# Base inverse step of a chunked delta-rule kernel as four fused multiply-adds, one a token tile, in place of one product and one sum over all four tiles

## The reference

```python
def _gated_delta_rule(q, k, v, g, beta):
    ...
    a_mat = jnp.where(strict, jnp.einsum('bhncd,bhnsd->bhncs', k_beta, k) * decay, 0.0)
    eye = jnp.eye(CHUNK, dtype=a_mat.dtype)
    t_mat = lax.linalg.triangular_solve(eye + a_mat, jnp.broadcast_to(eye, a_mat.shape),
                                        left_side=True, lower=True)
    u = jnp.einsum('bhncs,bhnse->bhnce', t_mat, v * beta[..., None])
    w = jnp.einsum('bhncs,bhnsd->bhncd', t_mat, k_beta * jnp.exp(g)[..., None])
    ...
    def step(s, inp):
        q_c, k_c, u_c, w_c, qk_c, gt = inp
        v_new = u_c - jnp.einsum('bhcd,bhde->bhce', w_c, s)
        o = jnp.einsum('bhcd,bhde->bhce', q_c, s) + jnp.einsum('bhcs,bhse->bhce', qk_c, v_new)
        s = s * gt[..., None, None] + jnp.einsum('bhcd,bhce->bhde', k_c, v_new)
        return s, o
```

## Time and profile before

| | |
|---|---|
| median of 3 runs | 1106.7 us (1106.35 to 1107.34) |
| the profiled execution | 1106.26 us, its span 1104.1 us |
| TensorE busy | 1068.6 us, 97% of the span |
| VectorE busy | 688.1 us, 62% |
| ScalarE busy | 532.2 us, 48% |
| mean granted TensorE clock | 0.995 |

### The profile page before, as it was taken

How to read it: one execution, slowest core, us unless ns; L and a number is a source line. 1 busy time by engine, 2 the same in 40 slices (tenths; PEclk the granted TensorE clock), 3 DMA queues, 4 the chain that set the end, 5 groups by cost and what they waited for, 6 DMA issues and landing times. The chain is left out here.

```text
span 1104.1 us, 19488 instructions
## 1 busy us (share of the span) xinstructions
PE 1068.6 (97%) x7212; PEld 848.8 (77%) x7212; DVE 688.1 (62%) x2078; ACT 532.2 (48%) x1557; POOL 121.7 (11%) x160
## 2 busy tenths in 40 slices
PE   7999999989999999999999999999999999999997
PEld 5877777767878787777877878787786878787775
DVE  5285959575655747576365765748456575758554
ACT  4556665644736444363354536344454546463300
POOL 3513122123200000020000000002000000002320
PEclk9999999999999999999999999999999999999999
DMA  8957475655652726253562551724544353612332
GB/s 278 315 202 258 167 264 193 240 181 182 227 195 87 243 83 228 89 183 98 175 203 110 194 180 58 249 74 157 156 151 153 126 160 119 229 62 75 115 104 87
DMA packets 58285, 183.54 MB, mean 166 GB/s; under 512 B 8464, under 2 KB 21200, under 8 KB 44880
## 3 DMA queue, kind: packets, MB, share of 16 engines
q1 hardware_dynamic: 51392, 173.13, 45.4%
q10 hardware_dynamic: 6800, 9.18, 2.9%
HBM read 138.22 MB, written 44.07 MB: 165 GB/s over the span
## 5 line engine op out<-in xcount | busy, mean ns | idle before, releaser
L827 PE MATMUL bank<-xr,w 128*128 128x512 f32 x2496 | 656.4, 406 | 7.8 <-DVE xr L1527 7.8
L827 PEld LDWEIGHTS bank<-xr,w 128*128 128x128 f32 x2496 | 450.5, 189 | 103.1 <-issue 10.6
L878 PE MATMUL bank<-wo,y_split 128*128 128x512 f32 x432 | 114.4, 404 | 0.0
L878 PEld LDWEIGHTS bank<-wo,y_split 128*128 128x128 f32 x432 | 77.0, 189 | 14.6 <-issue 0.7
L1575 DVE SCALAR_TENSOR_TENSOR kq<-conv_in,convw_all,kq 128x512 f32<-128x512 f32 x96 | 76.1, 794 | 8.6 <-ACT conv_in L1169 6.4
L1478 ACT ACTIVATE o_scaled<-bank 128x128 f32<-128x128 f32 x64 | 17.7, 276 | 125.6 <-PE bank L1099 125.3
L1331 ACT ACTIVATE score<-score,neg_max 128x256 f32<-128x256 f32 (+1 forms) x128 | 62.7, 493 | 17.6 <-DVE neg_max L1747 17.6
L1781 DVE TENSOR_TENSOR y_step<-blocks,y_cols 128x60 f32<-128x60 f32 (+14 forms) x240 | 49.9, 208 | 20.0 <-DMA blocks<-n_spill 11.7
L1909 DVE TENSOR_SCALAR steps<-bank,nb_rk 128x128 f32<-128x128 f32 x64 | 22.3, 348 | 64.2 <-PE bank L1095 64.2
L1912 DVE SCALAR_TENSOR_TENSOR state<-state,cols_all,bank 128x128 f32<-128x128 f32 x64 | 22.2, 347 | 62.7 <-PE bank L1098 62.7
L761 POOL TENSOR_TENSOR xr<-y_tile,xr 128x256 fp32r<-128x256 f32 x8 | 6.0, 772 | 457.0 <-ACT xr L1150 457.0
(11 more groups left out here) (217 smaller groups left out, 1637.3 us busy)
## 6 DMA issues: line engine op xcount, KB each, us to landing
w<-w_split SPq DMA_DIRECT2D x78, 1024.0 KB, 5.6
w_split<-w SPq DMA_DIRECT2D x26, 1024.0 KB, 4.9
blocks<-n_spill ACTq DMA_DIRECT2D x32, 256.0 KB
y_spill<-y_out SPq DMA_DIRECT2D x30, 256.0 KB, 5.4
x_tile<-w_in SPq DMA_DIRECT2D x13, 512.0 KB, 5.8
y_tile<-w_in SPq DMA_DIRECT2D x12, 512.0 KB, 5.9
y_tile<-y_spill SPq DMA_DIRECT2D x12, 512.0 KB, 6.2
x_tile<-x SPq DMA_DIRECT2D x12, 512.0 KB, 3.9
```

The lines of the kernel that those rows point to most:

```text
L827: ins = nc.tensor.matmul(bank[JOBS[at].bank][:], w[:, turn % 3, wp, k, :], xr[:, xp, k], start=(step == 0), stop=(step == 3 * KT - 1))
L878: ins = nc.tensor.matmul(bank[JOBS[at].bank][:], y_place(t)[:, yp, k], wo[:, k, wp, half * UNIT:(half + 1) * UNIT], start=(step == 0), sto ...
```

## The change

A step j of the base inverse is four SCALAR_TENSOR_TENSOR instructions, one for each tile c, each of which multiplies by `y_cols[:, c, j]` (one value per partition) and adds in one pass. `y_step` is no longer used here. The even tiles wait on `base_step`: tile 0 for tiles 0 and 1 of the step before, tile 2 for tiles 2 and 3 of it. The odd tiles and all tiles of step 0 do not wait on it.

```diff
-        base_step = counter("base_step", 2 * (BASE - 1))
+        base_step = counter("base_step", CH * (BASE - 1))
...
                     rest = slice(j + 1, BASE)
-                    wide = [P, CH, BASE - 1 - j]
-                    if j > 0:
-                        after(dve, base_step, n, 2 * j)
-                    nc.vector.tensor_tensor(y_step[:, :, rest], blocks[:, j, :, j + 1:],
-                                            y_cols[:, :, j:j + 1].to_broadcast(wide), ALU.mult).then_inc(base_step.sem, 1)
-                    after(dve, base_step, n, 2 * j + 1)
-                    start = ident16[:, rest].unsqueeze(1).to_broadcast(wide) if j == 0 else y_cols[:, :, rest]
-                    nc.vector.tensor_tensor(y_cols[:, :, rest], y_step[:, :, rest], start, ALU.add).then_inc(base_step.sem, 1)
-                after(dve, base_step, n, 2 * (BASE - 1))
+                    for c in range(CH):
+                        if j > 0 and c % 2 == 0:
+                            after(dve, base_step, n, CH * (j - 1) + c + 2)
+                        start = ident16[:, rest] if j == 0 else y_cols[:, c, rest]
+                        nc.vector.scalar_tensor_tensor(y_cols[:, c, rest], blocks[:, j, c, rest], y_cols[:, c, j:j + 1], start,
+                                                       ALU.mult, ALU.add).then_inc(base_step.sem, 1)
+                after(dve, base_step, n, CH * (BASE - 1))
```

## The result

The changed kernel takes 1125.3 us (median of 4 runs, 1124.1 to 1129.7) against 1107.0 for the kernel before, measured beside it (4 runs, 1106.4 to 1107.5). The ratio is 1.0179, 95% interval 1.0158 to 1.0200; the quotient of the two medians, 1.0165, lies inside it. The forecast was 1123, with a range of 1109 to 1130. The profiled execution took 1125.6 us, with a span of 1123.5, 19.4 more than before.

The account below looks back on a forecast made before the run. TensorE was taken as the bound, so VectorE's change counts only where TensorE waits at L1045 for the transpose. 1.61 us a slot, less free delay and stalls, sums to 16.6; 1106.26 + 16.6 = 1122.9, predicted 1123, range 1109 to 1130.

Parts of the forecast that it names:

- Free-running instructions and their price: VectorE's base_inverses: no even tile waits, so 60 instructions cost their free-running spacing, 8.47 us a slot against 6.87.
- the fixed part: Share of a VectorE instruction's spacing that is there whatever its length: 0.131 us with a per-partition scalar, bounds 0.066 and 0.131.
- Rival 4: VectorE's base_inverses: every second instruction held until its predecessor has written, 11.7 us a slot, 1167 us; chance 0.04.
- rival 1: VectorE's base_inverses: the per-partition scalar costs nothing in the stream, 4.6 us instead of 6.87, 1098 us; chance 0.10.
- All of the delay counts: TensorE at L1045: delay beyond each slot's free share is added in full, neither caught up nor counted twice; 16.6 us.
- the 16.6 us: Sum over the 16 slots of the delay of TensorE's weight load L1045 behind the transpose.
- Rival 3: Half of the delay is absorbed as TensorE's later waits in the slot shrink: about +8, 1115 us; chance 0.10.
- the late slots: Slots 12, 13, 14: TensorE waits and a stall hides the first half's loss, so 3 x 0.95 = 2.9 us.
- TensorE's own busy time stays: Sign in the profile: TensorE's busy time, 1068.6 us before, does not change.
- GpSimd's share: Slots 0 to 2: GpSimd's subtraction may slow one more short instruction, about 0.5 us each, 1.6 in all, outside the sum.
- the stall at j = 8: Function's wait for the second half of blocks; in slots 4, 12, 13, 14 it hides the first half's 0.66 us.
- The small signs: VectorE's busy time rises by 25 to 35 us; L1045's wait rises to about 30 us in 14 or 15 slots.

Follow-up runs that it names:

- Experiment 1: Changed kernel with the per-partition scalar replaced by a constant, count, length and order of instructions kept: 1095.8 us, ratio 0.9903.
- experiments 2 and 3: Kernel before with eight, then four, short products behind the last step, a delay of 1.6 or 0.8 us a slot: 1130.7 and 1117.5 us.
- before, convs behind (7): Kernel before with the convolutions convs(n, 0.2) moved behind base_inverses: 1108.2 us, ratio 1.0004.
- two chains, convs behind (8): Kernel before with wide instructions cut into two alternating chains and the convolutions moved behind base_inverses: 1105.6 us, ratio 0.9988.
- two chains, early convs (9): Kernel before with two alternating chains and the convolutions moved behind base_inverses in slots 0 to 2 alone: 1102.7 us, ratio 0.9947.
- two chains (5): Kernel before with each wide instruction cut into two pairs of tiles in alternating chains, 60 plain instructions a slot: 1101.8 us, ratio 0.9956.
- later place (4): Changed kernel with the places of the lowest level in the slot moved back, more dense matmuls ahead of L1045: 1126.5 us, ratio 1.0180.
- after, convs behind (6): Changed kernel with the convolutions convs(n, 0.2) moved behind base_inverses: 1124.0 us, ratio 1.0139.
- after, GpSimd done (10): Changed kernel in which slots 0 to 2 wait for the last of GpSimd's subtractions before the function begins: 1132.0 us, ratio 1.0214.

## Why the prediction was right, point by point

**Free-running instructions and their price.** Held. No even tile waited, the fixed part was 0.130 for a forecast of 0.131, the function 8.38 us for 8.47. Rival 4 (every second one held, 11.7 us a slot) is out. Experiment 1 shows the other branch: with a constant the fixed part is 0.070 and the time 1095.8, near rival 1's 1098. The Trainium skill, Vector Engine (DVE) Microarchitecture Reference, section Measured stream behaviour on trn2, gives about 75 ns per instruction; this case agrees for instructions without a per-partition scalar (0.070) and not for those with one (0.130).

**All of the delay counts.** Right in direction and as the cause, as experiments 2 and 3 show: the pure delay reproduces the loss, and half the delay loses about half. But the 16.6 us were said to be idle time of TensorE, and that grew by 11.1 only; the other 8.3 are the clock. Rival 3's time (half absorbed, 1115) is out; its mechanism, smaller waits later in the slot, shows as no more than 1.7 us (L1045's wait grew by 12.8, TensorE's idle time by 11.1). How much later L1045 comes in each slot than before, beyond the slot before (from its weight loads; 1.58 for slot 0 is 79.88 - 78.30):

```
slots                   forecast   measured
0, 1, 2, 3, 7, 11       9.7        1.58 + 2.79 + 3.43 + 2.70 + 1.76 + 1.83 = 14.1
12, 13, 14              2.9        0.12 - 1.82 - 0.91 = -2.6
4                       0.6        2.7
5, 6, 9, 10             2.4        0.53 + 0.49 + 0.52 + 0.68 = 2.2
8                       0.0        1.3
15                      1.0        0.9
to L1045 of slot 15     16.6       18.6 (0.8 more from there to the end)
```

About 6 of the 14.1 us in the first line are busy time of TensorE, as are the 1.3 of slot 8, so the waiting in the six slots of the first line came to about 8 for the forecast 9.7. Two terms were missed, with opposite signs: the clock (+8.3) and the late slots (-2.6 for +2.9). That the total came within 3 us is in part luck.

**Missed: the clock.** "TensorE's own busy time stays" failed: 1076.9 for 1068.6, +8.3 us, nearly half of the loss. Over all the profiles the same 7212 matmuls take the longer, the lower the granted clock, and on the whole, though not in each pair, the clock is lower where L1045 waits longer (us of wait for the transpose, granted clock, TensorE's busy us):

```
constant (1)                 3.2    0.998   1066.3
before, convs behind (7)     7.1    0.997   1067.6
two chains, convs behind (8) 8.2    0.996   1067.8
two chains, early convs (9) 10.5    0.994   1069.7
two chains (5)              12.1    0.995   1069.1
before                      13.4    0.995   1068.6
later place (4)             18.3    0.991   1073.2
delay of 0.8 (3)            20.0    0.993   1073.0
after, convs behind (6)     20.2    0.987   1076.6
after                       26.2    0.987   1076.9
delay of 1.6 (2)            29.0    0.982   1082.2
after, GpSimd done (10)     32.6    0.985   1077.5
```

In the kernels before and after every stretch at a low clock inside the slots stands right behind a wait for the transpose, two before and six after. The trace that the prediction was made from had the sign of it: the wait of 3.00 us in slot 3 has a granted clock of 0.66 over the 5 us behind it. Of the increments above, those of slots 1 to 3 hold the most of it: slot 1 came 2.79 us later where 1.6 had been said, 1.5 of that as busy time, slot 2 3.43 later with 2.8 of it. Of L1045's waits the shortest with a lower clock right behind it was 1.87 us, but longer ones left the clock at 1.00: 2.33 us ahead of slot 11 and 2.89 ahead of slot 4, 2.94 and 2.92 in experiment 10 and, before the change, 2.19 ahead of slot 13. In slot 2 of experiments 4 and 6 the clock fell to 0.50 for some us behind another wait, 1.05 us for the attention weights (L950), after several waits close together. So the length of the wait alone does not decide it; what else does is not settled here.

**GpSimd's share: as named in slots 0 to 2, and overlooked in slot 3.** Beside GpSimd the first four instructions take 1.6 us more than in slot 5 in slot 0 and 1.0 more in slots 1 and 2, and experiment 10 shows the cause. But the old function had lost 1.0 us to it in each of these slots as well. From its first start to the spreading product it went from 7.85 to 9.98 us in slot 0, from 7.85 to 9.43 in slot 1 and from 7.84 to 9.42 in slot 2. That is 2.1, 1.6 and 1.6 more, where the prediction had 1.61 and up to 0.5 on top. Slot 3, which the prediction did not name here, stands under GpSimd too: the function takes 10.54 us there before and 12.72 after, 2.2 more, beside two groups of four instructions of GpSimd. During the second group 7 of the new instructions run, in the equally long stretch behind it 23, with the DMA engines busy in both (first GpSimd's second group; then two stretches, their us, the busy us and count of these VectorE instructions, the clock, the DMA share and GB/s):

```profile
242.36 2.86 POOL L761 TENSOR_TENSOR wo<-x_tile,wo 128x256 fp32r<-128x256 f32 x4 [0.99 <-ACT wo L1164]
...
242.36:245.22 2.86, 2.86 (x7) 1.00 1.01 337
245.22:248.08 2.86, 2.86 (x23) 1.00 0.83 328
```

This is the slot with the longest wait of L1045, 3.00 us before and 5.14 after.

**Missed: the late slots.** In slots 12 to 14 the forecast let the stall at j = 8 stand and fall by 0.66 us. It was nearly gone (0.29 us at step 8 of slot 12, none in slot 13), and the three slots gave back 2.6 us instead of costing 2.9. The stall moved about in every run: the idle time of the function for `blocks` is 11.7 us before, 4.8 after, 7.4 with the delay of 1.6 and 14.0 with the constant. The prediction had also left out that the start waited for the first half of `blocks` in slots 4, 12, 13 and 14, 0.9 to 1.3 us each, 4.4 of the 11.7 us before; behind such a wait VectorE being late costs nothing either. In slot 4 it went the other way: the start waited 3.13 us (0.94 before), step 8 only 0.27:

```profile
314.09 0.67 DVE L1782 SCALAR_TENSOR_TENSOR y_cols<-blocks,y_cols,ident 128x15 f32<-128x15 f32 x4 [3.13 <-DMA blocks<-n_spill]
```

A landing taken from one execution is no fixed point for another. Why the blocks land when they do in these slots was not tested, and it leaves some us of experiment 10 and of the late slots unexplained.

**The small signs.** VectorE's busy time rose by 42 us, not 25 to 35: the waiting pairs had left more small gaps than I had counted. In slot 5 the function went from 5.77 to 8.35 us busy, and 16 times that difference is 41. L1045's wait came to 26.2 us in 15 slots where about 30 in 14 or 15 had been said.

## What to carry to other kernels

Fusing a product and a sum pays by what an instruction costs in the stream, not by the number of operations: here, at 1 to 15 elements, one with a per-partition scalar costs about 0.14 us and one with a constant 0.08, and each of a dependent chain of wide ones 0.20 to 0.25. So 30 wide held instructions (6.87 us) beat 60 fused ones (8.38), and 60 plain ones in two alternating chains (6.47) beat both. When a delay lands on a wait of TensorE, add to it what TensorE loses in clock behind the longer wait; here that put 8.3 us on top of 11.1 of idle time. And read the slots one by one for what else runs beside the changed code: slot 3 had the longest wait before the change, and GpSimd ran beside the function there.

## What the runs showed of the hardware

- A per-partition scalar operand costs a short SCALAR_TENSOR_TENSOR 0.06 us of stream time over a constant (0.130 against 0.070 fixed), at 1 to 15 elements.
- The granted clock of TensorE fell to 0.51 over 6.7 us behind a wait of 2.56 us and to 0.59 over 4.1 us behind one of 2.80; over the run TensorE was busy 8.3 us longer, of 19.4 in all. Behind waits of 2.89 and 2.94 us it stayed at 1.00.
- Four short two-source instructions of VectorE took 2.25 and 1.70 us beside GpSimd's subtraction and 0.67 without it; in slot 3 seven of them ran in 2.86 us beside it and 23 in the 2.86 us behind it.
- Two alternating chains start two held instructions in the 0.20 us in which one chain starts one.
